# Sample attention of a hybrid decoder step: a batch's values move from behind the next batch's second quad of pages to behind its first, and ScalarE issues its pages one by one

## The chip, the cores and the metric

The kernel runs on one core of a Trainium2 chip. The metric is the device time of one execution in microseconds; the time before is the median of three runs.

## The reference, cut to what matters

The program is one inference step of a decoder layer (RWKV7 heads and MLA heads side by side, cross attention to a memory, a convolutional FFN) for a prompt of 1024 tokens and a sample group of 8 sequences with 4 new tokens each. The change concerns only the MLA attention of the sample group over its paged cache:

```python
lat_past = cache_mla_latent[l][page_table].reshape(Bs, past_len, KV_LORA)   # 8 x 2048 x 256
kr_past = cache_mla_krope[l][page_table].reshape(Bs, past_len, QK_ROPE)     # 8 x 2048 x 32
q_abs = jnp.einsum('bthd,chd->bthc', q_nope, w_uk)
sc_past = jnp.einsum('bthc,bsc->bhts', q_abs, lat_past) + jnp.einsum('bthr,bsr->bhts', q_rope, kr_past)
sc = jnp.concatenate([sc_past.astype(jnp.float32) * MLA_SCALE, sc_new], axis=-1)
pr = jax.nn.softmax(sc, axis=-1).astype(lat_new.dtype)
o_lat = (jnp.einsum('bhts,bsc->bthc', pr[..., :P], lat_past)
         + jnp.einsum('bhts,bsc->bthc', pr[..., P:], lat_new))
```

A sequence ("batch" in the code, 8 of them) has 16 pages of 128 positions. 8 heads times 4 tokens make 32 query rows.

## The kernel before

The kernel is a chain of stages, each a block in which every engine has a program of its own, written out by hand and tied to the others by semaphores; a stage begins when all engines have left the one before. The sample attention is `mla_sample_stage`. All is in float32.

Pages come by DMA into `keys` (latents) and `kr` (rotated keys), which hold two batches, `b % 2`. Three queues issue them, SyncE's, GpSimd's and ScalarE's; `LOADED` says which of the 16 pages each takes. Each page costs the issuing engine a load of the page's number from the table (`value_load`) and two issues, 16 KB of `kr` and 128 KB of `keys`. The pages of batch b+1 overwrite those of batch b-1, so all three wait for `o_made`, which TensorE counts up at the end of `outputs(b-1)`.

Four pages make a quad, four quads a batch. For quad n of batch b TensorE runs

- `transposes(b, n)`: eight 128x128 transposes of latents into two PSUM banks,
- `rope_keys(b, n)`: one transpose of the quad's rotated keys into slot n of the bank `xb`,
- `scores(b, n)`: the products with the queries, after ScalarE has copied the transposed quad out (`copy_keys`, two copies, and `copy_rope`, one).

When all four quads of batch b have scores, a chain follows that goes from engine to engine: VectorE takes the maximum (`maximum`, L1196 to L1200), TensorE spreads it over the partitions (`spread_maxima`, L1040 and L1041), VectorE reduces it (L1204), ScalarE takes the exponentials (`exponential`, L1136 and L1138), TensorE transposes them (`probabilities`, L1048 and L1050, into the same bank `xb`, all four slots), ScalarE copies them (`copy_probabilities`, L1143), and TensorE multiplies them with the pages (`outputs`, "the values", L1059 and L1061). VectorE copies the result (L1216), TensorE turns it (`turn_outputs`, L1066 and L1068), and VectorE scales it (L1218, L1221).

Each engine takes its instructions in the order of its program. Before the change TensorE's order for a batch b after the first is: quad 0 transposed; the last scores of b-1; quad 1 transposed; `spread_maxima(b-1)`; scores of quad 0; `probabilities(b-1)` and `outputs(b-1)`; quad 2 transposed; scores of quad 1; `turn_outputs(b-1)`; quad 3 transposed; scores of quad 2. ScalarE's order is: copies of quads 0 and 1; exponentials and copy of the probabilities of b-1; copies of quad 2; its three pages of batch b+1, all at once; copies of quad 3.

VectorE has other work in this stage. After the outputs of b-1 are scaled, it runs `shift` for two of the 14 tiles of RWKV's token shift (L1185 to L1191, two instructions over 1056 columns and two small ones each), and only then comes `maximum(b)`. There is no shift in the last batch.

Of the kernel before, what the change touches and what calls it, by code (L numbers as in the profile page):

```python
# [24 lines left out]
TP, NB, TSEQ = 1024, 8, 4  # L25
# [15 lines left out]
NPG = PAST // PAGE  # L41
# [850 lines left out]
def mla_sample_stage(k, free_y, free_cq, qabs, qrope):  # L892
# [7 lines left out]
    nc, io = k.nc, k.io  # L900
    R = NH * TSEQ
    GP, GC, NQ = 4, 4 * PAGE, NPG // 4
# [2 lines left out]
        "tr_made", "tr_taken", "t_made", "t_taken", "s_made", "gm", "rm", "dm", "b_made", "m_ready", "e_done", "l_sum", "l_diag",  # L905
        "pn_made", "pn_taken", "pt_made", "pt_taken", "o_made", "o_taken", "ot_made", "r_done", "ot_taken", "uv_made")}

    LOADED = (0, 2, 5, 8, 10, 13, 15), (1, 4, 6, 9, 12, 14), (3, 7, 11)
    k_in = [[[k.sem(f"ms_k{e}{j}{g}") for g in range(NQ)] for j in range(2)] for e in "spa"]
    loads = [[2 * sum(n in mine for n in range(GP * g, GP * (g + 1))) for g in range(NQ)] for mine in LOADED]  # L910
    B = k.bank
    lat = k.cqkv[:, QK:QK + KK, :]
# [7 lines left out]
    with ExitStack() as ctx:  # L920
# [3 lines left out]
        pages = k.sb(ctx, "ms_pages", [1, NB * NPG], I32)  # L924
# [21 lines left out]
        o_tr, l_ps = yb[:, 384:384 + KK * R], yb[:, 448:448 + R]  # L946
        query = lambda kk, b: qabs[:, kk, b, :, :].rearrange("p h t -> p (h t)")

        def load_batch(eng, e, b, j):
            for n in LOADED[e]:  # L950
                page = eng.value_load(pages[0:1, bass.ds(b * NPG + n, 1)], min_val=0, max_val=io["lat"].shape[0] - 1)
                eng.dma_start(kr[:, j, n, :], io["kr"][bass.ds(page, 1)].rearrange("a p c -> p (a c)"))\
                   .then_inc(k_in[e][j][n // GP], 16)
                eng.dma_start(keys[:, j, n, :], io["lat"][bass.ds(page, 1)].rearrange("a p c -> p (a c)"))\
                   .then_inc(k_in[e][j][n // GP], 16)

        def load_keys(eng, e):
            eng.wait_ge(S["pg"], 16)

            def load(b, j):  # L960
                load_batch(eng, e, b, j)
            load(0, 0)
            load(1, 1)
            with eng.Fori(1, NB // 2) as i:
                for j in range(2):

                    eng.wait_ge(S["o_made"], 2 * i + j - 1)
                    load(2 * i + j, j)
        with nc.Block() as block:
# [17 lines left out]
            def _(pe):  # L987
# [12 lines left out]
                def transposes(b, n):  # L1000
                    j, i = b % 2, NQ * b + n
                    for e in range(3):

                        pe.wait_ge(k_in[e][j][n], 16 * loads[e][n] * (b // 2 + 1))
                    if i >= 2:
                        pe.wait_ge(S["t_taken"], 2 * (i - 1))
                    for kk in range(KK):
                        for g in range(GP):
                            mm = pe.transpose(B[2 * (n % 2) + kk][:, g * PAGE:(g + 1) * PAGE],
                                              keys[:, j, GP * n + g, kk * P:(kk + 1) * P], ident)  # L1010
                        mm.then_inc(S["t_made"], 1)

                def rope_keys(b, n):
                    i = NQ * b + n
                    if i:
                        pe.wait_ge(S["tr_taken"], i)
                    if b and n == 2:
                        pe.wait_ge(S["pt_taken"], b)
                    pe.transpose(xb[:, n * P:(n + 1) * P],
                                 kr[:, b % 2, GP * n:GP * (n + 1), :].rearrange("p a c -> p (a c)"), ident).then_inc(S["tr_made"], 1)  # L1020

                def scores(b, n):
                    j, i, ps = b % 2, NQ * b + n, sbank[b % 2]
                    if n == 0 and b >= 2:
                        pe.wait_ge(S["e_done"], 2 * (b - 1))
                    pe.wait_ge(S["tr_taken"], i + 1)
                    pe.wait_ge(S["t_taken"], 2 * (i + 1))
                    c = slice(n * PAGE, (n + 1) * PAGE)
                    for kk in range(KK):
                        for g in range(GP):  # L1030
                            pe.matmul(ps[g * R:(g + 1) * R, c], query(kk, b), kT[:, n % 2, kk, g * PAGE:(g + 1) * PAGE],
                                      start=(kk == 0), stop=False, skip_group_check=True)
                    pe.matmul(ps[:, c], qd[:, b, :, :].rearrange("p g r -> p (g r)"), krT[:, j, c], start=False, stop=True,
                              skip_group_check=True).then_inc(S["s_made"], 1)
# [8 lines left out]

                def probabilities(b):
                    j = b % 2
                    pe.wait_ge(S["tr_taken"], NQ * b + 6 if b < NB - 1 else NQ * NB)
                    pe.wait_ge(S["e_done"], 2 * (b + 1))
                    pe.transpose(pn_ps, sc[:, j, GC:], ident).then_inc(S["pn_made"], 1)  # L1048
                    for n in range(NQ):
                        mm = pe.transpose(xb[:, n * P:(n + 1) * P], sc[:, j, n * PAGE:(n + 1) * PAGE], ident)  # L1050
                    mm.then_inc(S["pt_made"], 1)
# [20 lines left out]
                pe.wait_ge(S["nk"], 1)  # L1072
                pe.wait_ge(S["big"], 1)
                for b in range(NB):
                    transposes(b, 0)
                    rope_keys(b, 0)
                    if b:
                        scores(b - 1, NQ - 1)
                    transposes(b, 1)
                    rope_keys(b, 1)  # L1080
                    if b:
                        spread_maxima(b - 1)
                    else:
                        pe.wait_ge(S["qd"], GP)
                    scores(b, 0)
                    if b:
                        probabilities(b - 1)
                        outputs(b - 1)
                    transposes(b, 2)
                    rope_keys(b, 2)  # L1090
                    scores(b, 1)
                    if b:
                        turn_outputs(b - 1)
                    transposes(b, 3)
                    rope_keys(b, 3)
                    scores(b, 2)
                scores(NB - 1, NQ - 1)
                spread_maxima(NB - 1)
                probabilities(NB - 1)
# [11 lines left out]
            @block.scalar  # L1111
            def _(act):
                act.activation(kr0[:, :], k.krope[64:96, TP:T], ACT.Copy).then_inc(S["kr0"], 1)
                act.wait_ge(S["pg"], 16)
                load_batch(act, 2, 0, 0)
                act.wait_ge(S["qd_zero"], 1)
                for g in range(GP):
                    act.activation(qd[g * R:(g + 1) * R, :, g, :], qrope[:, :, :, :].rearrange("p b h t -> p b (h t)"), ACT.Copy)\
                       .then_inc(S["qd"], 1)

                def copy_keys(b, n):
                    i = NQ * b + n
                    for kk in range(KK):
                        act.wait_ge(S["t_made"], KK * i + kk + 1)
                        act.activation(kT[:, n % 2, kk, :], B[2 * (n % 2) + kk], ACT.Copy).then_inc(S["t_taken"], 1)

                def copy_rope(b, n):
                    act.wait_ge(S["tr_made"], NQ * b + n + 1)
                    act.activation(krT[:, b % 2, n * P:(n + 1) * P], xb[:, n * P:(n + 1) * P], ACT.Copy).then_inc(S["tr_taken"], 1)

                def exponential(b):
                    j = b % 2
                    act.wait_ge(S["m_ready"], b + 1)
                    if b:
                        act.wait_ge(S["l_sum"], b)
                    act.activation(sc[:, j, 0:GC], sbank[j], ACT.Exp, bias=stat[:, 2:3], scale=SCALE, accum_out=stat[:, 3:4])\  # L1136
                       .then_inc(S["e_done"], 1)
                    act.activation(sc[:, j, GC:], nsc[:, b * R:(b + 1) * R], ACT.Exp, bias=stat[:, 2:3], scale=SCALE,  # L1138
                                   accum_out=stat[:, 4:5]).then_inc(S["e_done"], 1)

                def copy_probabilities(b):
                    act.wait_ge(S["pt_made"], b + 1)
                    act.activation(pT[:, :], xb, ACT.Copy).then_inc(S["pt_taken"], 1)  # L1143
                load_batch(act, 2, 1, 1)
                act.wait_ge(S["nsc"], 1)
                for b in range(NB):
                    for n in range(NQ):
                        if b and n == 2:
                            exponential(b - 1)
                            copy_probabilities(b - 1)  # L1150
                        copy_keys(b, n)
                        copy_rope(b, n)
                        if n == 2 and 1 <= b < NB - 1:
                            act.wait_ge(S["o_made"], b)
                            load_batch(act, 2, b + 1, (b + 1) % 2)
                exponential(NB - 1)
                copy_probabilities(NB - 1)

# [1545 lines left out]
```

## Time and profile before

| | |
|---|---|
| time, median of 3 runs | 2604.76 us (2602.73 to 2605.34) |
| profiled execution, its own time | 2603.54 us |
| span of the profile | 2601.9 us |
| sample attention stage | about 605 to 757 us of the span |
| TensorE busy over the span | 2280.0 us (88%) |
| mean granted TensorE clock | 0.918 of full speed |

The profile gives times from the start of the span. Busy time of TensorE is its matrix products with modelled ends; "idle before" in a row is the time in which the engine did nothing before that instruction, with what ended it.

### The profile page before, as it was taken

What the parts mean: (1) busy time and instruction counts of PE and PEld (TensorE: products, weight loads), DVE (VectorE), ACT (ScalarE), POOL (GpSimd) and SP (SyncE); (2) the same over time, 40 slices, a digit from 0 to 9 for tenths busy, and PEclk for the clock granted to TensorE, in tenths of its full rate; (3) what the DMA queues carried; (4) which work ended last, traced back from release to release, by engine and by line L of the source; (5) the groups of instructions that cost most, each with busy time, mean ns of one, the idle gap of its engine ahead of it and who ended that gap; (6) DMA issues with size and microseconds to landing.
All of it is one profiled execution on the core that took longest, in us unless ns stands there. A gap on an engine that the chain in (4) does not pass through costs nothing. (4 is left out here: it accounts for less than half of the span.)

```text
span 2601.9 us, 51029 instructions
## 1 busy us (share of the span) xinstructions
PE 2280.0 (88%) x20442; PEld 2073.2 (80%) x20442; DVE 1317.5 (51%) x2428; ACT 649.8 (25%) x1340; POOL 285.6 (11%) x225
## 2 busy tenths in 40 slices
PE   5999589997763999977877899798999999999994
PEld 5999367776541899953776898798999999999994
DVE  5111644443547555535634224355666666666667
ACT  3000233443431444410223012112122222111212
POOL 2333000003313000000310310130000000000000
PEclk9999799998985999975898898899999999999997
DMA  3110100004520000010314124201111111111112
GB/s 131 49 45 27 37 11 11 11 1 112 145 60 0 8 4 4 4 40 0 123 41 131 71 73 148 79 33 55 49 48 43 49 50 49 50 41 50 33 33 73
DMA packets 79018, 131.55 MB, mean 51 GB/s; under 512 B 26705, under 2 KB 56274, under 8 KB 78706
## 3 DMA queue, kind: packets, MB, share of 16 engines
q1 hardware_dynamic: 67698, 117.12, 13.6%
q0 software_dynamic: 4224, 8.13, 1.2%
q10 hardware_dynamic: 6912, 3.54, 0.5%
q8 instruction: 153, 2.51, 0.4%
q14 instruction: 31, 0.25, 0.0%
HBM read 119.48 MB, written 9.29 MB: 49 GB/s over the span
## 5 line engine op out<-in xcount | busy, mean ns | idle before, releaser
L345 PE MATMUL psum<-high,ff_up 128*128 128x352 f32 x2112 | 517.5, 326 | 4.9 <-DVE ff_u L2439 3.1
L345 PEld LDWEIGHTS psum<-high,ff_up 128*128 128x128 f32 x2112 | 370.6, 189 | 7.1 <-DVE ff_u L2439 4.3
L345 PE MATMUL psum<-low,ff_up 128*128 128x352 f32 x1056 | 341.1, 323 | 0.0
L345 PE MATMUL psum<-hid,ff_down 128*128 128x352 f32 x1584 | 259.6, 325 | 12.1 <-issue 12.1
L345 PEld LDWEIGHTS psum<-hid,ff_down 128*128 128x128 f32 x1584 | 258.0, 189 | 12.4 <-issue 12.4
L345 PE MATMUL psum<-h_high,pj_part 128*128 128x352 f32 x960 | 236.0, 327 | 30.4 <-POOL pj_part L396 24.7
L345 PEld LDWEIGHTS psum<-low,ff_up 128*128 128x128 f32 x1056 | 199.5, 189 | 0.0
L345 PEld LDWEIGHTS psum<-h_high,pj_part 128*128 128x128 f32 x960 | 172.1, 192 | 31.1 <-POOL pj_part L396 24.7
L2484 DVE TENSOR_TENSOR x<-x,psum 128x352 f32<-128x352 f32 x264 | 137.2, 521 | 114.8 <-PE psum L345 114.8
L345 PE MATMUL psum<-h_low,pj_part 128*128 128x352 f32 x480 | 157.7, 328 | 0.0
L2334 ACT ACTIVATE ff_up<-ff_slot 128x1024 fp32r<-128x1024 f32 x44 | 46.2, 1051 | 390.9 <-PE psum L345 384.7
L345 PE MATMUL psum<-high,wo_part 128*128 128x352 f32 x384 | 95.7, 331 | 12.1 <-POOL wo_part L396 11.1
L345 PE MATMUL psum<-m_high,mo_part 128*128 128x352 f32 x384 | 94.9, 329 | 9.5 <-POOL mo_part L396 9.5
L2365 ACT ACTIVATE ff_c<-ff_u,vecs 128x1072 f32<-128x1072 f32 x44 | 56.5, 1285 | 185.8 <-DVE ff_u L2439 146.9
L345 PE MATMUL psum<-m_high,mq_part 128*128 128x352 f32 x384 | 95.2, 330 | 3.9 <-POOL mq_part L396 3.9
L1484 PE MATMUL psum<-rc_W 64*64 64x64 f32 x1296 | 90.5, 222 | 3.5 <-DVE rc_W L1592 2.6
L486 DVE TENSOR_TENSOR rw<-psum,acc 128x352 f32 x42 | 22.1, 526 | 140.4 <-PE psum L345 140.4
L345 PEld LDWEIGHTS psum<-h_low,pj_part 128*128 128x128 f32 x480 | 91.9, 191 | 0.1
L716 PEld LDWEIGHTS psum<-mp_v,mp_pT 128*128 128x128 f32 x576 | 71.8, 195 | 21.3 <-issue 11.4
L716 PE MATMUL psum<-mp_v,mp_pT 128*128 128x64 f32 x576 | 76.2, 279 | 7.0 <-ACT mp_pT L787 7.0
L345 PEld LDWEIGHTS psum<-high,wo_part 128*128 128x128 f32 x384 | 68.9, 193 | 13.5 <-POOL wo_part L396 12.2
L834 DVE TENSOR_REDUCE mp_stat<-psum 128x1 f32<-128x128 f32 (+3 forms) x64 | 48.4, 756 | 58.0 <-PE psum L696 57.9
(395 smaller groups left out, 4605.2 us busy)
## 6 DMA issues: line engine op xcount, KB each, us to landing
ff_slot<-in_w_up SPq DMA_DIRECT2D x44, 512.0 KB, 3.3
ff_slot<-in_w_down SPq DMA_DIRECT2D x22, 512.0 KB, 3.2
pj_slot<-in_w_in SPq DMA_DIRECT2D x20, 512.0 KB, 3.2
mk_slot<-in_w_mkv SPq DMA_DIRECT2D x16, 512.0 KB, 3.3
mz_k<-in_memk SPq DMA_DIRECT2D x8, 1024.0 KB, 5.5
mz_v<-in_memv SPq DMA_DIRECT2D x8, 1024.0 KB, 7.5
ms_keys<-in_lat SPq DMA_DIRECT2D x56, 128.0 KB, 2.7
ms_keys<-in_lat POOLq DMA_DIRECT2D x48, 128.0 KB, 3.0
```

What stands on the lines that cost most here:

```text
L345: mm = pe.matmul(ps, w(a, kk), rhs(b, kk), start=(kk == 0 and n == 0), stop=(kk == nk - 1 and n == 2))
L486: return eng.tensor_tensor(dst[:, bass.ds(m, 1), n * C3:(n + 1) * C3], ps.unsqueeze(1), third(k.acc, n).unsqueeze(1), ALU.mult)
L716: mm = pe.matmul(B[6][:, 0:HD], pT[:, i % 2, t * P:(t + 1) * P], v[:, t, h * HD:(h + 1) * HD], start=(t == 0), stop=(t == i))
L834: dve.reduce_max(mx[:, i:i + 1], ps, AX).then_inc(S["maxed"], 1)
L1484: mm = pe.matmul(PV[hf][h, at(64 * q)], W[h, p, N_, :], W[h, p, TT_, :], start=True, stop=True)
L2334: act.activation(dst[:, 0], slot[:, j], ACT.Copy).then_inc(S["w_high"], 1)
L2365: act.activation(cv[:, j, :], u[:, j, 2:U], ACT.Identity, bias=k.vecs[:, bass.ds(b0, 1)], scale=k.vecs[:, bass.ds(w2, 1)]).then_inc(S["c_f ...
L2484: dve.tensor_tensor(xs, xs, B[4 + g % 4][:, 0:C3], ALU.add).then_inc(S["down_taken"], 1)
```

## The change

On TensorE the last scores of batch b-1 and `spread_maxima(b-1)` come first, ahead of quad 0 of batch b. Then quad 0 is transposed, and `probabilities(b-1)` and `outputs(b-1)` follow at once. Quad 1 is transposed after them, then come the scores of quad 0 and `turn_outputs(b-1)`, and quads 2 and 3 in the plain order. On ScalarE the exponentials of b-1 come ahead of the copies of quad 0, and the copy of the probabilities behind them. Its three pages of b+1 are issued one each behind the copies of quads 1, 2 and 3. Pages are dealt to the queues anew: ScalarE's are 7, 11 and 15 (3, 7 and 11 before), SyncE and GpSimd share the others. The semaphore values follow the new order: `probabilities(b)` waits for the rope copy of quad 0 of b+1 (quad 1 before).

```diff
-    LOADED = (0, 2, 5, 8, 10, 13, 15), (1, 4, 6, 9, 12, 14), (3, 7, 11)
+    LOADED = (0, 2, 4, 6, 9, 12, 14), (1, 3, 5, 8, 10, 13), (7, 11, 15)
...
-                    if b and n == 2:
+                    if b and n == 1:
                         pe.wait_ge(S["pt_taken"], b)
...
-                    pe.wait_ge(S["tr_taken"], NQ * b + 6 if b < NB - 1 else NQ * NB)
+                    pe.wait_ge(S["tr_taken"], NQ * b + 5 if b < NB - 1 else NQ * NB)
...
                 for b in range(NB):
+                    if b:
+                        scores(b - 1, NQ - 1)
+                        spread_maxima(b - 1)
                     transposes(b, 0)
                     rope_keys(b, 0)
                     if b:
-                        scores(b - 1, NQ - 1)
+                        probabilities(b - 1)
+                        outputs(b - 1)
+                    else:
+                        pe.wait_ge(S["qd"], GP)
                     transposes(b, 1)
                     rope_keys(b, 1)
-                    if b:
-                        spread_maxima(b - 1)
-                    else:
-                        pe.wait_ge(S["qd"], GP)
                     scores(b, 0)
                     if b:
-                        probabilities(b - 1)
-                        outputs(b - 1)
-                    transposes(b, 2)
-                    rope_keys(b, 2)
-                    scores(b, 1)
-                    if b:
                         turn_outputs(b - 1)
-                    transposes(b, 3)
-                    rope_keys(b, 3)
-                    scores(b, 2)
+                    for n in range(2, NQ):
+                        transposes(b, n)
+                        rope_keys(b, n)
+                        scores(b, n - 1)
...
                 for b in range(NB):
-                    for n in range(NQ):
-                        if b and n == 2:
-                            exponential(b - 1)
-                            copy_probabilities(b - 1)
+                    if b:
+                        exponential(b - 1)
+                    copy_keys(b, 0)
+                    copy_rope(b, 0)
+                    if b:
+                        copy_probabilities(b - 1)
+                    for n in range(1, NQ):
                         copy_keys(b, n)
                         copy_rope(b, n)
-                        if n == 2 and 1 <= b < NB - 1:
-                            act.wait_ge(S["o_made"], b)
-                            load_batch(act, 2, b + 1, (b + 1) % 2)
+                        if 1 <= b < NB - 1:
+                            if n == 1:
+                                act.wait_ge(S["o_made"], b)
+                            load_page(act, 2, b + 1, (b + 1) % 2, LOADED[2][n - 1])
```

`load_page` is the body of the old `load_batch` for one page.

## Rows read from the trace of the kernel before

**Rows 1.** The page of the profile, its first line.

```profile
span 2601.9 us, 51029 instructions
```

**Rows 2.** Busy time of each engine, six batches' period and the stage's end.

```profile
core 0: us, PE busy (x) PEld busy (x) DVE busy (x) ACT busy (x) POOL busy (x), PEclk, DMA share, GB/s
...
632.30:735.20 102.90, 80.34 (x944) 59.52 (x943) 51.04 (x114) 40.09 (x102) 38.70 (x72) 0.97 0.53 141
735.20:756.50 21.30, 15.55 (x160) 10.84 (x159) 4.82 (x17) 4.19 (x11) 0.00 (x0) 0.73 0.09 21
```

**Rows 3.** Waits of TensorE, 632.3 to 735.2: us, times, longest.

```profile
PE psum L1009 <- DMA ms_keys<-in_lat: 8.4, 6, 2.5
...
PE psum L1009 <- ACT ms_kT L1125: 2.1, 1, 2.1
```

**Rows 4.** Timeline of one undisturbed period: start, us, engine line op, idle before.

```profile
667.20 1.09 PE L1009 MATMUL psum<-masks,ms_keys 128*128 128x128 f32 x8
667.31 0.43 DVE L1216 COPY ms_ol<-psum 128x256 f32<-128x256 f32 x1 [3.50 <-PE psum L1061]
667.89 1.08 ACT L1125 ACTIVATE ms_kT<-psum 128x512 f32<-128x512 f32 x2 [3.33 <-PE psum L1009]
...
668.86 0.28 ACT L1129 ACTIVATE ms_krT<-psum 128x128 f32<-128x128 f32 x1
...
669.23 0.31 PE L1066 MATMUL psum<-ms_ld,masks 128*128 128x32 f32 x2
...
670.62 1.25 DVE L1185 TENSOR_TENSOR sh_tmp<-rw 128x1055 f32<-128x1055 f32 x1
...
676.08 0.68 DVE L1196 TENSOR_REDUCE ms_stat<-psum 128x1 f32<-128x512 f32 x1
...
678.43 0.69 ACT L1136 ACTIVATE ms_sc<-psum,ms_stat 128x512 f32<-128x512 f32 x1
...
679.65 0.27 PE L1048 MATMUL psum<-masks,ms_sc 128*32 128x128 f32 x1 [0.59 <-ACT ms_sc L1138]
...
681.14 1.93 PE L1059 MATMUL psum<-ms_keys,ms_pT 128*32 128x256 f32 x32 [0.78 <-ACT ms_pT L1143]
...
683.73 0.42 DVE L1216 COPY ms_ol<-psum 128x256 f32<-128x256 f32 x1 [3.50 <-PE psum L1061]
```

**Rows 5.** Timeline of a period that waited for pages.

```profile
639.31 1.97 PE L1009 MATMUL psum<-masks,ms_keys 128*128 128x128 f32 x8 [2.27 <-DMA ms_keys<-in_lat]
...
643.00 0.69 DVE L1196 TENSOR_REDUCE ms_stat<-psum 128x1 f32<-128x512 f32 x1 [1.79 <-PE psum L1033]
```

**Rows 6.** ScalarE's page issues in the timeline.

```profile
669.11 0.34 ACTq L952 DMA_DIRECT2D ms_kr<-in_kr  x1
...
670.67 0.34 ACTq L952 DMA_DIRECT2D ms_kr<-in_kr  x1
```

**Rows 7.** GpSimd's second page in the timeline, and landing time of latent pages.

```profile
671.01 0.54 POOL L954 DMA_DIRECT2D ms_keys<-in_lat  x1
```

```profile
DMA to landing us min/median/max: 2.0/3.0/4.3
```

**Rows 8.** Timeline of the last batch's chain.

```profile
741.00 0.69 DVE L1196 TENSOR_REDUCE ms_stat<-psum 128x1 f32<-128x512 f32 x1 [2.32 <-PE psum L1033]
...
742.26 0.49 PE L1040 MATMUL psum<-ms_dm,masks 128*128 128x128 f32 x2 [1.30 <-DVE ms_dm L1200]
...
744.56 0.27 PE L1048 MATMUL psum<-masks,ms_sc 128*32 128x128 f32 x1 [1.59 <-ACT ms_sc L1138]
...
746.23 3.64 PE L1059 MATMUL psum<-ms_keys,ms_pT 128*32 128x256 f32 x32 [0.78 <-ACT ms_pT L1143]
...
751.06 0.42 DVE L1216 COPY ms_ol<-psum 128x256 f32<-128x256 f32 x1 [5.91 <-PE psum L1061]
```

**Rows 9.** Stretches of 1 us; the columns are those of rows 2.

```profile
639.00:640.00 1.00, 0.69 (x3) 0.69 (x4) 0.96 (x4) 0.72 (x3) 0.54 (x2) 0.57 0.59 136
...
708.00:709.00 1.00, 0.18 (x2) 0.19 (x3) 1.00 (x2) 0.82 (x2) 0.20 (x2) 1.00 0.68 191
```

More of the change, by code:

```diff
@@ L947, in mla_sample_stage, with load_page @@
         query = lambda kk, b: qabs[:, kk, b, :, :].rearrange("p h t -> p (h t)")
[L949 to L955, printed above, removed]
+        def load_page(eng, e, b, j, n):
+            page = eng.value_load(pages[0:1, bass.ds(b * NPG + n, 1)], min_val=0, max_val=io["lat"].shape[0] - 1)
+            eng.dma_start(kr[:, j, n, :], io["kr"][bass.ds(page, 1)].rearrange("a p c -> p (a c)"))\
+               .then_inc(k_in[e][j][n // GP], 16)
+            eng.dma_start(keys[:, j, n, :], io["lat"][bass.ds(page, 1)].rearrange("a p c -> p (a c)"))\
+               .then_inc(k_in[e][j][n // GP], 16)
         def load_keys(eng, e):
@@ L960, in load @@
             def load(b, j):
-                load_batch(eng, e, b, j)
+                for n in LOADED[e]:
+                    load_page(eng, e, b, j, n)
             load(0, 0)
@@ L1114, in _ @@
                 act.wait_ge(S["pg"], 16)
-                load_batch(act, 2, 0, 0)
+                for n in LOADED[2]:
+                    load_page(act, 2, 0, 0, n)
                 act.wait_ge(S["qd_zero"], 1)
@@ L1143, in copy_probabilities @@
                     act.activation(pT[:, :], xb, ACT.Copy).then_inc(S["pt_taken"], 1)
-                load_batch(act, 2, 1, 1)
+                for n in LOADED[2]:
+                    load_page(act, 2, 1, 1, n)
                 act.wait_ge(S["nsc"], 1)
                 for b in range(NB):
-                    for n in range(NQ):
-                        if b and n == 2:
-                            exponential(b - 1)
-                            copy_probabilities(b - 1)
+                    if b:
[5 more added lines that the diff above has]
+                    for n in range(1, NQ):
                         copy_keys(b, n)
                         copy_rope(b, n)
-                        if n == 2 and 1 <= b < NB - 1:
-                            act.wait_ge(S["o_made"], b)
-                            load_batch(act, 2, b + 1, (b + 1) % 2)
+                        if 1 <= b < NB - 1:
+                            if n == 1:
+                                act.wait_ge(S["o_made"], b)
+                            load_page(act, 2, b + 1, (b + 1) % 2, LOADED[2][n - 1])
                 exponential(NB - 1)
```

## Prediction

> **What bounds the kernel now.** I read the first line of the page for the span to which all is added [rows 1], then cut the stage into stretches with the view of busy time, listed TensorE's waits in the middle stretch, and followed one period instruction by instruction in the timeline. Nothing outside the stage is touched, and the next stage starts when this one ends, so what the stage gains or loses the program gains or loses.
>
> The stretch from 632.3 to 735.2 us runs from the copy of batch 0's outputs to that of batch 6: six periods in 102.9 us, a mean of 17.15 us, of which TensorE is busy 13.4 us [rows 2]. So TensorE stands still for 3.8 us a period. Of those 22.6 us in all, 8.4 us are waits for pages and 2.1 us one wait for ScalarE's copies, which its page issues held up [rows 3]. The rest is the chain: each period it waits 0.59 us for the exponentials and 0.78 us for the copied probabilities [rows 4].
>
> The reader should see two halves in a period. I count from the copy of the outputs (v, 667.31 us), which is when pages may be loaded. The first half ends at VectorE's maximum at 676.08 us, 8.77 us later. That row has no idle before it: VectorE comes straight from the two shifts that began at 670.62 us, so in an undisturbed period VectorE's shifts, not the pages, say when the maximum starts. The second half is the chain from the maximum to the next copy of outputs at 683.73 us, 7.65 us. Together 16.42 us [rows 4]. In a period disturbed by pages the maximum came at 643.00 us, 10.7 us after v at 632.3, and did wait for TensorE [rows 2, 5]. Two periods are of this kind; four of nearly 16.5 us and two of 18.4 us make the 102.9.
>
> **What the change takes away.** Pages of b+1 are still issued from v on, but the values are now ahead of quad 1, so at v three quads of b are left instead of two, before b+1 is touched. The fourth page of a batch is now GpSimd's second; that issue came 3.7 us after v, and with the longest landing time of 4.3 us it is there at v + 8.5 [rows 4, 7]. TensorE asks for it only behind the maximum's spreading, at about v + 10.6 (below). The page waits go, 8.4 us. What they were worth is less: it is the excess of the two disturbed periods, 2 x 1.9 = 3.8 us, since in the others VectorE would not have started earlier anyway.
>
> **ScalarE's pages.** Issues of consecutive pages are 1.56 us apart [rows 6]. One page between two quads' copies therefore makes ScalarE's quad about 2.1 us (0.5 us until the second copy is under way and its sequencer is free, and 1.6), against TensorE's quad of 2.03 us (667.20 to 669.23) [rows 4]. It holds the last scores up by 0.1 us or so, at most by one issue, 1.6 us, if an issue is slow. The last scores end near v + 7.7 and VectorE is free at v + 8.77, so 1.0 us of it is covered by the shifts. I take nothing.
>
> **What the change puts on the path.** VectorE's order is unchanged. `turn_outputs` still comes one quad behind the values, hence the shifts still begin 3.3 us after v and the maximum still starts at v + 8.77. The shifts that were half hidden by page waits are now the bound of every first half.
>
> The second half gets longer. `probabilities` overwrites the bank `xb`, in whose slot 0 the rope keys of b+1's first quad stand, and so waits for their copy. ScalarE now makes the three copies of that quad behind the exponentials. In the period shown, exponentials start at 678.43 and `probabilities` at 679.65. Between the two there will now stand one set of copies, from 667.89 to 668.86 + 0.28 = 1.25 us [rows 4]. A copy of this quad cannot be earlier: ScalarE's program has it behind `exponential`. The lower bound is 1.2 us and the upper, if TensorE's transposes of the quad are late too, 1.9. I take 1.22, at the lower end: the quad is transposed 1.8 us after the spreading begins, and the exponentials end only 2.2 us after it. The second half is then 7.65 + 1.22 = 8.87 us, and the period 8.77 + 8.87 = 17.64 us.
>
> Six periods: 6 x 17.64 = 105.8 against 102.9: +2.9 us. The last batch has no shift, but at v one more quad is left than before: +2.03 us [rows 4]. In batch 0 the last scores now come ahead of a quad, which starts the chain some 1.0 us sooner, and the 1.2 us of copies follow: +0.2 us. The end of the stage, from the last maximum at 741.00 us on, is as it was. Sum at an unchanged clock: +5.1 us.
>
> **The clock.** TensorE now stands still while the chain runs. Before, quads lay in the gaps; now, from the end of the last scores (v + 7.6) it waits 2.4 us for the maximum (v + 8.77, and 1.26 us more to the spreading, as 741.00 to 742.26 shows [rows 8]), works 1.8 us on the spreading and quad 0, waits some 1.7 us for the copies, works 0.7 us and waits 0.8 us. About 4.9 us of 7.5 are idle, every batch.
>
> The trace shows what such stretches do. Before the disturbed period TensorE was idle for 2.27 us; the granted clock sank from 1.00 within that microsecond (mean 0.57), and the eight transposes took 1.97 us instead of 1.09 [rows 5, 9]. In the last batch it waited 1.30 us and 1.59 us with the spreading between; the products of the values then ran at 1.2 GHz, 3.64 us instead of 1.93, and from their start to the copy of the outputs went 4.83 us instead of 2.59 [rows 4, 8]. Against that stands the wait of 2.1 us, after which the clock was still 1.00 [rows 3, 9]; but quads ran on both sides of it. The new period has a longer gap than any of these and a second one 1.8 us of work later. So I expect the clock to fall in nearly every batch.
>
> What a fall costs depends on what it covers. If only the spreading and quad 0: the transposes take 0.9 us more, part of it behind the exponentials, so about 0.6 us. If the values: 4.83 - 2.59 = 2.2 us. If both and the quad after: 2.2 + 0.6 with some 0.5 for the first transposes, about 3. Seven batches have this chain with a quad in it (0 to 6). Both kinds should occur; in the middle between 0.6 and 2.2, 1.5 us each, so 7 x 1.5 = +10.5 us (bounds +4 and +21).
>
> The Trainium skill, "TensorE: Matmul & The Clock Gate", speaks to this in two places. Its section "HAM oscillation" ties a fall to a single long wait of TensorE, longer than any gap worked out above; by it there would be none here and +5.1 us would stay. The trace speaks against it: the clock fell behind a wait of 2.27 us. Its section "A second HAM failure mode: psum-queue depth-cycling" says that frequent short idling between groups of matmuls is enough to make the clock swing; the falling clock in the last batch agrees.
>
> **The sum.** Against the profiled execution: its span is 2601.9 us and its time 2603.54, the median is 1.2 us more than that time. +5.1 and +10.5 make +15.6 us: 2619.1 for the profiled execution, 2620.4 against the median of 2604.76. Slower by 0.6%.
>
> **The rivals.**
> (a) The clock holds: 2609.9 us, just inside 0.2%. For it: the wait of 2.1 us that it survived. Against it: both falls above, and two gaps in each period. Chance 0.15.
> (b) The shifts do not hold the maximum up. Then the first half is about 7.7 us, the period 16.6, six periods 99.5: 3.4 us won, 2.2 lost at both ends, 2603.6 at an unchanged clock. Against it: no idle before the maximum's row in the undisturbed period, and VectorE's order is untouched. Chance 0.05.
> (c) Faster: the copies of quad 0 stay off the path between exponentials and probabilities, because TensorE and ScalarE pass it while VectorE is still at work. This is worth 6 x 1.22 = 7.3 us, and the period would be 16.42; with 2.0 us lost at the end 6 x 16.42 = 98.5 gives -4.4 + 2.0 = -2.4 us, and with (b) as well -8.6 us, 2596.2. It turns faster by 0.2% only from 0.5 us less per period than 16.42. The program order on ScalarE and the wait for `xb` stand against it. Chance 0.03.
> (d) The change does not do what it says: page waits remain, since pages came up to 2.5 us late before [rows 3]. They would have to exceed the 2 us of reserve for quad 0 and add to the forecast: 2625 us. Within the forecast's range.
>
> **Chances and range.** Forecast 0.77 (with (d)), its own range 2611 to 2628. Below 2608 lie (b) and (c), above 2629 falls that cover the values and more in every batch: together under 0.2. Range 2608 to 2629. A measurement of this kernel can tell about 0.2%, 5.2 us, from no change. Faster: (c), 0.03. Same: (b) and a little over half of (a), 0.14. Slower: 0.83.
>
> **What would show it.** In the new profile: waits of TensorE for pages near zero between batch 0's and batch 6's outputs; a period of 17.6 us plus what the clock costs, so that the stretch of six becomes 112 to 120 us; VectorE's maximum again 8.8 us after the copy of outputs, with no idle before it; ScalarE's copies of quad 0 straight behind the exponentials, and TensorE waiting for the rope copy ahead of `probabilities`, some 1.7 us; `spread_maxima` behind a wait of 2.4 us for VectorE; and a granted clock under 1.00 in the chain of most batches, with values taking up to 3.64 us. The prediction is wrong if the clock stays at 1.00 in the stretch, or if the maximum starts well before v + 8.77.

## The result, and the profile after

The changed kernel takes 2611.85 us (median of 20 runs, 2603.87 to 2621.09) against 2600.39 us for the kernel before (20 runs on the same chips, 2592.19 to 2608.41): 11.5 us more, ratio 1.0045 with a 95% interval of 1.0035 to 1.0054. It is slower, as forecast, and inside the range. The forecast difference was 15.6 us. The absolute time forecast, 2620.4 us, also stood on the first three runs of before, whose median is 4.4 us over that of all 20.

```profile
span 2606.6 us, 51030 instructions
```

The profiled execution is 4.7 us longer than that of before [rows 1], which hides more than it shows. From VectorE's first use of the new tokens' scores to its last copy of the stage went 147.8 us before (608.04 to 755.85) and 157.4 us now (604.17 to 761.53), 9.6 us more. The stage began 3.9 us earlier, by an earlier stage that the change doesn't touch, and what follows the stage took 1.0 us less. So I read the stage, and take the whole from the medians.

The view of busy time, from the copy of batch 0's outputs to that of batch 6; columns as in [rows 2]:

```profile
630.07:739.22 109.15, 82.27 (x943) 60.91 (x944) 50.91 (x115) 39.49 (x102) 38.55 (x72) 0.94 0.52 137
```

Six periods take 109.15 us instead of 102.9, and the granted clock is 0.94 instead of 0.97. The waits of TensorE from 623 to 740 us:

```profile
PE psum L1040 <- DVE ms_dm L1203: 15.5, 7, 2.4
PE psum L1048 <- ACT ms_krT L1127: 9.7, 7, 1.7
PE psum L1059 <- ACT ms_pT L1141: 5.4, 7, 0.8
```

This list answers to [rows 3]. All waits for pages are gone, 8.4 us of them. In their place stand 15.5 us for VectorE's maximum ahead of the spreading and 9.7 us for the rope copy ahead of `probabilities`. These count seven chains; in the six periods of [rows 3] alone the two are 14.2 and 8.0 us. A period in which the clock held, in the timeline (compare [rows 4]; VectorE's and ScalarE's line numbers have moved by a few):

```profile
648.10 0.42 DVE L1219 COPY ms_ol<-psum 128x256 f32<-128x256 f32 x1 [3.50 <-PE psum L1061]
...
656.87 0.68 DVE L1199 TENSOR_REDUCE ms_stat<-psum 128x1 f32<-128x512 f32 x1
...
658.12 0.49 PE L1040 MATMUL psum<-ms_dm,masks 128*128 128x128 f32 x2 [2.36 <-DVE ms_dm L1203]
...
659.20 0.69 ACT L1134 ACTIVATE ms_sc<-psum,ms_stat 128x512 f32<-128x512 f32 x1 [4.55 <-DVE ms_stat L1207]
...
660.18 1.07 ACT L1123 ACTIVATE ms_kT<-psum 128x512 f32<-128x512 f32 x2
...
661.13 0.28 ACT L1127 ACTIVATE ms_krT<-psum 128x128 f32<-128x128 f32 x1
...
661.47 0.28 PE L1048 MATMUL psum<-masks,ms_sc 128*32 128x128 f32 x1 [1.65 <-ACT ms_krT L1127]
...
665.57 0.42 DVE L1219 COPY ms_ol<-psum 128x256 f32<-128x256 f32 x1 [3.50 <-PE psum L1061]
```

The maximum starts 8.77 us after the copy of outputs, to the hundredth what it was, and again without idle time before it. From there to the next copy of outputs go 8.70 us, 1.05 us more than in [rows 4], and the copies of quad 0 (660.18 to 661.41) stand in that stretch. The period is 17.47 us.

The other periods were 18.03, 19.11, 17.98 and 19.09 us. What they have more, 4.3 us in all, is falls of the granted clock from 2.4 to 1.2 GHz. Two of them in the timeline; the answers in before are the fall in [rows 8] and the slow transposes in [rows 5]:

```profile
640.15 0.79 PE L1040 MATMUL psum<-ms_dm,masks 128*128 128x128 f32 x2 [2.40 <-DVE ms_dm L1203]
...
641.16 1.91 PE L1009 MATMUL psum<-masks,ms_keys 128*128 128x128 f32 x8
...
735.00 3.03 PE L1059 MATMUL psum<-ms_keys,ms_pT 128*32 128x256 f32 x32 [0.78 <-ACT ms_pT L1141]
...
739.22 0.42 DVE L1219 COPY ms_ol<-psum 128x256 f32<-128x256 f32 x1 [5.11 <-PE psum L1061]
```

Behind a gap of 2.40 us the spreading took 0.79 us instead of 0.49 and quad 0 took 1.91 us; such a period is 0.5 us longer. Where the fall came later, the values took 3.03 us instead of 1.93, and the period is 1.6 us longer. The granted clock in one microsecond of those values is 0.50 (columns as in [rows 2]):

```profile
737.00:738.00 1.00, 1.00 (x13) 0.19 (x5) 0.00 (x0) 0.00 (x0) 0.00 (x0) 0.50 0.68 150
```

### The profile page after: what moved, and what is told of

The parts are those of the page before. It is cut to its first block and busy times, and to the rows that moved or that the text cites. A ratio compares the mean times of both kernels' runs of the same rounds, so it can differ in the third digit from the quotient of the medians.

```text
span 2606.6 us, 51030 instructions
## 1 busy us (share of the span) xinstructions
PE 2277.4 (87%) x20442; PEld 2070.9 (79%) x20442; DVE 1317.4 (51%) x2428; ACT 648.6 (25%) x1340; POOL 285.5 (11%) x225
## 3 DMA queue, kind: packets, MB, share of 16 engines
q1 hardware_dynamic: 67698, 117.12, 13.5%
## 5 line engine op out<-in xcount | busy, mean ns | idle before, releaser
L345 PEld LDWEIGHTS psum<-hid,ff_down 128*128 128x128 f32 x1584 | 257.8, 189 | 12.4 <-issue 12.4
```

The lines of the kernel that those rows point to most:

```text
L345: mm = pe.matmul(ps, w(a, kk), rhs(b, kk), start=(kk == 0 and n == 0), stop=(kk == nk - 1 and n == 2))
```

## The experiments

Theory: VectorE's shifts fix the first half of a period, the copies of quad 0 lengthen the second, and with no quads left inside the chain TensorE's clock falls in it. Rivals: pages or ScalarE's issues still hold the kernel; the loss is all waits and the clock costs nothing; what matters is how ScalarE issues. Every kernel was measured beside the kernel before on its chip. The ratios are to that, and "before us" is its median there.

| run | median us | before us | ratio (95%) | copies of outputs of batches 0 to 6, us |
|---|---|---|---|---|
| the change | 2611.85 | 2600.39 | 1.0045 (1.0035 to 1.0054) | 109.15 |
| e1, after, no reload | 2607.96 | 2598.51 | 1.0048 (1.0029 to 1.0068) | 109.44 |
| e2, before, no reload | 2609.40 | 2598.51 | 1.0042 (1.0028 to 1.0056) | 114.46 |
| e3, after, narrow filler | 2616.12 | 2598.51 | 1.0058 (1.0039 to 1.0077) | 111.74 |
| e4, after, quad 0 first | 2616.16 | 2598.51 | 1.0065 (1.0049 to 1.0080) | 118.15 |
| e5, after, shift moved | 2604.51 | 2600.49 | 1.0017 (0.9999 to 1.0035) | 106.56 |
| e6, before, shift moved | 2600.42 | 2600.49 | 0.9994 (0.9983 to 1.0005) | 105.42 |
| e7, after, issue in one | 2624.09 | 2600.49 | 1.0080 (1.0058 to 1.0102) | 128.32 |
| e8, before, issue one by one | 2604.71 | 2600.49 | 1.0007 (0.9995 to 1.0020) | 108.01 |
| e9, after, transposes in the gaps | 2599.68 | 2600.01 | 0.9996 (0.9982 to 1.0009) | 104.91 |
| e10, quad 0 first and shift moved | 2599.12 | 2600.01 | 0.9992 (0.9978 to 1.0005) | 103.18 |
| e11, e10 with transposes | 2586.54 | 2600.01 | 0.9945 (0.9926 to 0.9964) | 92.58 |
| e12, before, transposes | 2601.14 | 2601.06 | 0.9994 (0.9978 to 1.0009) | 103.99 |

**e1: are pages still on the path?**

```diff
-            with eng.Fori(1, NB // 2) as i:
-                for j in range(2):
-                    eng.wait_ge(S["o_made"], 2 * i + j - 1)
-                    load(2 * i + j, j)
...
-                        pe.wait_ge(k_in[e][j][n], 16 * loads[e][n] * (b // 2 + 1))
+                        pe.wait_ge(k_in[e][j][n], 16 * loads[e][n])
...
-                        if 1 <= b < NB - 1:
-                            if n == 1:
-                                act.wait_ge(S["o_made"], b)
-                            load_page(act, 2, b + 1, (b + 1) % 2, LOADED[2][n - 1])
```

> The changed kernel without the loads of pages for batches 2 to 7 on all three queues (and without their waits): it computes with the pages of batches 0 and 1 again. Theory (shifts on VectorE and the chain set the period, pages hidden): the time of the changed kernel, 11.5 us over before, within 2 us; periods of 17.5 us plus falls of the clock. Rival (pages or ScalarE's page issues still hold the changed kernel): 5 us or more faster than the changed kernel.

No. Without the reloads the ratio is the changed kernel's, and the six periods too. The maximum still starts at v + 8.77 us in each. Pages and ScalarE's issues are hidden in the changed kernel. (e1 and e2 compute with stale pages, so only their times mean anything.)

**e2: what were the page waits worth before?** The same edit on the kernel before.

> The kernel before, without the loads of pages for batches 2 to 7 (and without their waits): it computes with the pages of batches 0 and 1 again. Theory (waits for pages were worth only the excess of the late periods over the shifts on VectorE): periods of 16.4 us, 3.8 to 4.5 us faster than before. Rival (each wait of TensorE for pages was on the path): 10.5 us faster than before.

Both were wrong: taking the waits away cost 10.9 us. In the view of busy time the granted clock fell to 0.81 over the six periods:

```profile
622.52:736.98 114.46, 93.73 (x943) 66.82 (x944) 50.82 (x115) 40.40 (x102) 0.00 (x0) 0.81 0.02 5
```

and the timeline of one period says why:

```profile
672.89 0.49 PE L1035 MATMUL psum<-ms_dm,masks 128*128 128x128 f32 x2 [2.38 <-DVE ms_dm L1192]
...
677.19 3.64 PE L1054 MATMUL psum<-ms_keys,ms_pT 128*32 128x256 f32 x32 [0.78 <-ACT ms_pT L1138]
```

With pages at hand TensorE transposes quads 0 and 1 early and then waits 2.38 us for VectorE, which in four of the six periods still starts its maximum at v + 8.77 us (in the other two, behind a slow chain, at v + 10.3 and 10.6). Before, the idle time lay in waits ahead of quads, six for pages of 8.4 us in all [rows 3], and quad 1 stood between the maximum and the spreading. The idle time has moved into the chain, as in the changed kernel, and in four of the six periods the values ran at 1.2 GHz: 3.64 us. TensorE's waits in the six periods sum to 20.8 us against 22.6 us before, so here it counted more where the waiting lay than how much of it there was.

**e3: TensorE kept busy with narrow products.**

```diff
+                def fill(count):
+                    for _ in range(count):
+                        pe.matmul(B[3][:, 0:32], ident, ident[:, 0:32], start=True, stop=True, skip_group_check=True)
...
                         scores(b - 1, NQ - 1)
+                        fill(14)
                         spread_maxima(b - 1)
...
                     rope_keys(b, 0)
                     if b:
+                        fill(9)
                         probabilities(b - 1)
```

> The changed kernel with 14 products of 128x32 that nobody reads ahead of the spreading and 9 ahead of the probabilities, in a free bank, so that TensorE is busy in its two long gaps. Theory (falls of the clock make up what the median of the changed kernel has over the sum of its waits, 4 to 8 us): the clock stays at 1.00 in the six periods, each 17.5 us, and the time is 4 to 8 us under the changed kernel's, so 4 to 8 us over before. Rival (the whole loss is the chain and the shifts; the clock costs nothing): the time of the changed kernel, 11.5 us over before.

It did not do what it was made for. The filler overran the first gap, so that an undisturbed period was 18.1 us, and two falls remained in the six periods:

```profile
665.91 3.21 PE L1038 MATMUL psum<-masks 128*128 128x32 f32 x28
...
673.88 3.55 PE L1063 MATMUL psum<-ms_keys,ms_pT 128*32 128x256 f32 x32 [0.78 <-ACT ms_pT L1147]
```

The microseconds around the start of the values, columns as in [rows 2]:

```profile
673.00:674.00 1.00, 0.22 (x5) 0.15 (x8) 0.00 (x0) 0.60 (x1) 0.00 (x0) 1.00 0.00 0
674.00:675.00 1.00, 1.00 (x13) 0.58 (x12) 0.00 (x0) 0.00 (x0) 0.00 (x0) 0.52 0.00 0
```

TensorE has no gap in these rows but the last, 0.78 us ahead of the values, which the filler left open; the clock was still 1.00 while that gap lasted and fell to 1.2 GHz right behind it, in both falls. Whether the narrow products or the open gap let it fall can't be told from this run. By itself it left the clock's share open too; e9 goes further.

**e4: quad 0 into the gap ahead of the spreading.**

```diff
-                        spread_maxima(b - 1)
                     transposes(b, 0)
                     rope_keys(b, 0)
                     if b:
+                        spread_maxima(b - 1)
                         probabilities(b - 1)
...
-                    if b:
-                        exponential(b - 1)
                     copy_keys(b, 0)
                     copy_rope(b, 0)
                     if b:
+                        exponential(b - 1)
                         copy_probabilities(b - 1)
```

> The changed kernel with quad 0 of the next batch transposed ahead of the spreading of the maxima, and its copies on ScalarE ahead of the exponentials. Theory (copies of quad 0 between exponentials and probabilities cost 1.2 us a batch, and the gap of 2.4 us ahead of the spreading lets the clock fall): the second half of a period is 7.65 us instead of 8.7, the period 16.4 us, the time 2 us under before (14 us under the changed kernel). Rival 1 (pages of quad 0 are now asked for 7.7 us after the copy of outputs and are late): waits for pages of up to 1 us a batch come back, and where VectorE's shifts do not cover them the time is 2 to 4 us over before. Rival 2 (the copies cost nothing): the time of the changed kernel less the clock's share.

The copies left the path, yet the time is 17.65 us over before's. The six periods took 118.15 us at a mean clock of 0.80:

```profile
630.54:748.69 118.15, 95.64 (x943) 66.14 (x944) 50.87 (x114) 40.50 (x102) 38.55 (x72) 0.80 0.47 126
```

One chain:

```profile
682.15 0.49 PE L1040 MATMUL psum<-ms_dm,masks 128*128 128x128 f32 x2 [1.37 <-DVE ms_dm L1202]
...
684.45 0.37 PE L1048 MATMUL psum<-masks,ms_sc 128*32 128x128 f32 x1 [1.58 <-ACT ms_sc L1136]
...
686.45 3.64 PE L1059 MATMUL psum<-ms_keys,ms_pT 128*32 128x256 f32 x32 [0.78 <-ACT ms_pT L1141]
```

No wait is longer than 1.6 us, and no page is late. But between 1.37, 1.58 and 0.78 us of waiting there is only the spreading and five transposes, and the values took 3.64 us in five of the six periods and 3.39 in the other. In three periods the next quad ran at 1.2 GHz too, the last scores came late, and the maximum with them (v + 10.3 to 10.8 instead of 8.8). My expectation had the waits right and left out the clock.

**e5 and e6: VectorE's shifts.**

```diff
                         total(b - 1)
+                        if b < NB - 1:
+                            shift(2 * b, 0)
                         take_outputs(b - 1)
+                    else:
+                        shift(2 * b, 0)
                     if b < NB - 1:
-                        shift(2 * b, 0)
                         shift(2 * b + 1, 1)
```

> The changed kernel with the first of a batch's two shifts on VectorE ahead of the copy of outputs, in the time in which VectorE waits for the values; the second stays behind the scaled outputs. Theory (the two shifts set the start of the maximum 8.8 us after the copy of outputs, TensorE would be ready at 7.7): the maximum starts at 7.7 us, a period is 1.0 us shorter, six of them 6 us; the gap ahead of the spreading shrinks from 2.4 to 1.3 us, so falls of the clock become fewer; 6 to 9 us under the changed kernel, 2.5 to 5.5 over before. Rival (the shifts only fill a wait): the time of the changed kernel, 11.5 us over before.

> The kernel before with the same move of one shift. Theory: in its undisturbed periods TensorE ends the last scores only 0.3 us before the maximum starts, held by pages and copies, so it gains 0.3 us in each of four or five periods, 1 to 2 us under before. Rival (the shifts hold before by as much as the changed kernel): 6 us under before.

On the changed kernel the maximum now waits for TensorE, 7.7 us after the copy of outputs (664.32):

```profile
672.04 0.69 DVE L1199 TENSOR_REDUCE ms_stat<-psum 128x1 f32<-128x512 f32 x1 [1.60 <-PE psum L1033]
```

Its shortest period is 16.41 us, 1.06 less than 17.47, and the time is 7.3 us under the changed kernel's. Falls are left (the other periods are 16.9 to 19.4 us). On the kernel before, three maxima start 0.3 us sooner (v + 8.46 to 8.48), as the theory said, but the time does not show it: the ratio's interval runs from 4.4 us under to 1.3 us over before. The rival's 6 us is excluded, the theory's 1 to 2 us can't be told from none. So the shifts do set the first half in the new order, and in the old one pages and copies stand close behind them.

**e7 and e8: how ScalarE issues.** e7 puts the old split and the block of three issues back into the changed kernel:

```diff
-                        if 1 <= b < NB - 1:
-                            if n == 1:
-                                act.wait_ge(S["o_made"], b)
-                            load_page(act, 2, b + 1, (b + 1) % 2, LOADED[2][n - 1])
+                        if n == 1 and 1 <= b < NB - 1:
+                            act.wait_ge(S["o_made"], b)
+                            for m in LOADED[2]:
+                                load_page(act, 2, b + 1, (b + 1) % 2, m)
```

> The changed kernel with the old split of the pages over the queues and ScalarE's three pages issued at once behind the copies of quad 1. Only TensorE's order and ScalarE's order of copies are then changed. Theory (ScalarE's issues matter by the slack of 1.0 us of the shifts): the block of three issues takes 4.0 us, the copies of quad 2 start 1.5 us late, those of quad 3 follow at once and the last scores end at most 0.5 us later than in the changed kernel, all under the shifts; the time of the changed kernel within 2 us. Rival (issuing one by one is a gain of its own in this order): 1 us a batch, 6 us over the changed kernel.

> The kernel before with the new split of the pages and ScalarE's pages issued one each behind the copies of quads 2 and 3 and of the next batch's quad 0; TensorE's order as before. Theory: the copies of quad 3 are no longer 2.3 us late, but the pages of the next quad 0 (GpSimd's second now) land no earlier and TensorE asks for them as early as before, so at most the 2.1 us wait for copies goes; 0 to 3 us under before. Rival (ScalarE's block of issues was what held the old order): 6 us or more under before.

e7 was the largest miss: 12 us over the changed kernel, where I had expected nothing. The timeline:

```profile
652.76 1.78 ACTq L953 DMA_DIRECT2D ms_keys<-in_lat  x1
...
656.13 1.09 ACT L1123 ACTIVATE ms_kT<-psum 128x512 f32<-128x512 f32 x2 [5.54 <-PE psum L1009]
...
657.45 0.33 PE L1019 MATMUL psum<-masks,ms_kr 128*128 128x128 f32 x1 [1.99 <-ACT ms_krT L1127]
```

The view of busy time and TensorE's largest wait, both from the copy of batch 0's outputs to that of batch 6:

```profile
626.18:754.50 128.32, 99.94 (x943) 70.47 (x944) 51.40 (x115) 39.28 (x102) 38.70 (x72) 0.77 0.43 116
```

```profile
PE psum L1019 <- ACT ms_krT L1127: 8.8, 6, 2.0
```

In every one of the six periods TensorE stood in front of a quad until ScalarE had done with its three issues and copied, 0.92 to 1.99 us, where the changed kernel does not wait at all. The row above is the longest of them, with one issue of 1.78 us instead of 0.34; it is ScalarE's only issue over 0.6 us in these periods, so it is the block as such that holds the copies up, and the slow issue adds to it once. The maximum started 9.7 to 12.4 us after the copy of outputs, not at 8.77. The shortest period, 18.37 us, is 0.9 us over the changed kernel's 17.47, which makes 5.4 of the 19.2 us that the six periods are longer; the others are 20.8 to 24.4 us, and the mean clock is 0.77, so much of the loss came by the clock once more. How much was not separated.

So the one-by-one issue is a part of the change that pays, by 9 us going by the ratios (1.0080 and 1.0045) and 12 by the medians, but only in this order: on the kernel before it brings nothing that can be measured (e8: the interval runs from 1.3 us under to 5.2 over before). The wait for the copies is gone there, as the theory said, but TensorE's waits for pages grew from 8.4 to 14.6 us. e7 differs in the split of the pages too. That was not tried by itself, but TensorE has no wait for a page in the six periods of e7, so the split didn't hold it there.

**e9: TensorE kept busy with full transposes.** As e3, with

```diff
+                        pe.transpose(B[3][:, 0:P], ident, ident)
```

for the product, 17 times ahead of the spreading, 12 ahead of the probabilities, 5 ahead of the values. Nobody reads the bank's content.

```profile
634.05:738.96 104.91, 98.47 (x1147) 79.06 (x1148) 50.92 (x114) 39.59 (x102) 38.70 (x72) 1.00 0.53 141
```

The granted clock is 1.00 over the whole stretch and the periods are 17.47 to 17.53 us, each. The kernel does more work than the changed one, waits for the same things, and is 12 us faster (ratios 0.9996 and 1.0045). With the falls gone, all that the change had lost is won back.

That doesn't make the longer waits free. The kernel before has falls of its own, e9 has hardly any, and the comparison sets the one against the other. The mean granted clock over the whole program shows it: 0.9205 for before (mean of the 81 runs recorded beside the experiments), 0.9184 for the change, 0.9228 for e9. Among the runs of before, 0.001 less of it goes with 1.6 us more time. By that, as an estimate, e9 would be about 4 us over before at before's own clock, close to the +5.1 us that the prediction gave the waits. A single profiled pair can't show this: those of the change and of e9 took 2608.24 and 2606.59 us, 3.6 under and 6.9 over their medians.

**e10 and e11: a kernel that is faster than both.** e10 is e4 and e5 together, with pages 2 and 3 exchanged between ScalarE and SyncE. e11 adds 12 and 5 transposes ahead of probabilities and values.

```diff
-    LOADED = (0, 2, 4, 6, 9, 12, 14), (1, 3, 5, 8, 10, 13), (7, 11, 15)
+    LOADED = (0, 3, 5, 8, 10, 13, 15), (1, 4, 6, 9, 12, 14), (2, 7, 11)
...
                         spread_maxima(b - 1)
+                        fill(12)
                         probabilities(b - 1)
+                        fill(5)
```

> The changed kernel with both: quad 0 transposed ahead of the spreading with its copies ahead of the exponentials, and one shift moved ahead of the copy of outputs; page 2 goes to ScalarE and page 3 to SyncE, so that quad 0's pages are issued sooner. By the waits alone a period is 7.7 + 7.6 = 15.3 us, 13 us less for six than the changed kernel's 17.5. Theory (the chain now holds hardly any matrix work, and the clock falls in each batch for longer, as with quad 0 alone, where periods were 18 to 21 us): periods of 17 to 19 us, time 4 to 12 us over before. Rival (with the shift out of the way the gaps are short enough): periods of 15.3 to 16 us, time 6 to 10 us under before.

> The kernel of e10_quad0_and_shift with 12 unread transposes ahead of the probabilities and 5 ahead of the values. Theory (only the clock keeps that order from its 15.3 us): the clock stays at 1.00 in the six periods, 15.3 to 15.8 us each, so 92 to 95 us for six against 103 before; 6 to 10 us under before. Rival (pages of quad 0, asked for 7.6 us after the copy of outputs, are late): waits for pages in TensorE's rows of 0.5 to 2 us a batch, periods of 16 to 17.5 us, time from 6 us under before to 2 over.

The view of busy time over the six periods, e10 and then e11:

```profile
628.52:731.70 103.18, 86.81 (x943) 61.10 (x944) 48.59 (x110) 40.29 (x102) 38.57 (x72) 0.88 0.54 142
```

```profile
629.83:722.41 92.58, 87.26 (x1045) 68.02 (x1046) 48.61 (x111) 40.19 (x102) 38.57 (x72) 1.00 0.58 156
```

e10 has periods of 16.9 to 17.2 us at a clock of 0.88 (the first 18.2), the low end of the theory's, and ends level with before, not 4 us or more over it. e11 differs from it by the transposes alone and has 15.34 to 15.38 us after the first, 15.77, at a clock of 1.00: 13.5 us under before, more than the 6 to 10 expected. One of its chains:

```profile
668.67 0.69 DVE L1204 TENSOR_REDUCE ms_stat<-psum 128x1 f32<-128x512 f32 x1 [1.60 <-PE psum L1033]
...
672.24 0.27 PE L1052 MATMUL psum<-masks,ms_sc 128*32 128x128 f32 x1 [0.28 <-ACT ms_sc L1142]
...
673.72 1.93 PE L1063 MATMUL psum<-ms_keys,ms_pT 128*32 128x256 f32 x32 [0.23 <-ACT ms_pT L1147]
```

The sum by waits, 15.3 us, comes out to within 0.1 us once the clock is held, and pages are not late.

**e12: do such transposes help any order?** The kernel before with 4 and 5 of them in its two short gaps, in bank `B[1]`, which is free there.

> The kernel before with unread transposes in the two short gaps of its chain: 4 ahead of the probabilities and 5 ahead of the values, in a bank that is free there. Theory (before has quads between its gaps, its clock falls only behind late pages, where these transposes do not stand): falls as before, 0 to 2 us under before. Rival (unread transposes help any order by as much, 12 us as in the changed kernel): 6 us or more under before.

No: 0.9994, with an interval from 5.7 us under to 2.3 us over before; the theory's 0 to 2 us can't be told from none. The old order has quads in its chain, and its two longest periods, 18.3 and 19.0 us, are again those in which the maximum waited for a late TensorE, ahead of which these transposes do not stand.

## Why the prediction was right, point by point

- **VectorE's shifts bound the first half.** Right. v + 8.77 us in all six periods of the changed kernel and in e1; moving one shift takes 1.06 us off (e5).
- **Page waits go, and were worth 3.8 us only.** The waits went. Their worth, 3.8 us, is not shown: e2 can't tell it, because without them the clock fell more often. That the step could have no price apart from the clock was not seen.
- **ScalarE's single issues cost nothing.** Right for the change as made (e1). The sentence did not go on to say what the block of issues would have cost; e7 shows 9 to 12 us, falls of the clock included.
- **The copies of quad 0 on the path.** Forecast 1.22 us and a period of 17.64; measured 1.05 and 17.47. From the exponentials' start to `probabilities` go 2.27 us instead of 1.22: ScalarE is on to the copies after 0.98 us, so the hand-over to TensorE within the 1.22 is paid once, not twice.
- **The unchanged-clock sum, +5.1 us.** Its size fits, its parts don't. In the profiled stages e9, the changed kernel at full clock up to the last batch's chain, took 152.7 us (607.00 to 759.74) against 147.8: +4.9 us. Of these, 2.0 lie in the six periods (2.9 forecast), 2.7 ahead of the copy of batch 0's outputs (0.2 forecast) and 0.2 behind that of batch 6 (2.0 forecast: the quad that is left did bring the last maximum 1.97 us later, but the chain behind it was 1.1 us shorter than before's, and the rest of the stage 0.6 us). That they add up to the forecast is luck, and each rests on one profiled execution. By e9's ratio the new order is 4.7 us under to 2.3 us over before, since before pays for falls of its own; at equal clock the estimate above gives 4 us.
- **The clock, +10.5 us.** That the clock costs this much is shown by e9: 12 to 13 us, by medians and ratios. The profiled executions show less. The falls of the six periods cost 4.3 us, and the stages of the change and of e9 are 4.6 us apart: four falls at 0.5 or 1.6 us each, the two kinds that were forecast, in four of six periods instead of all. The price of one was right for the first kind (0.6) and 0.6 us too high for the second (2.2), since such a fall covered only a part of the values. What the falls were in the executions that make the medians can't be seen.
- **Rival (a), the clock holds.** Refuted. The Trainium skill, "TensorE: Matmul & The Clock Gate", section "HAM oscillation", ties falls to one long wait; here no wait of the six periods was over 2.40 us and the clock of e4 fell with none over 1.6 us. The section "A second HAM failure mode: psum-queue depth-cycling" of the same page of the Trainium skill, which names frequent short idling between groups of matmuls, agrees with both.
- **Rivals (b), (c), (d).** (b) and (c) did not occur, but both are reachable: e10 removes the shifts and the copies from the path, and e11 shows that 15.3 us is what is then left. (d) did not occur: TensorE has no wait for a page left.

By medians and ratios the first term came out some 6 us lower than forecast (-4.7 to +2.3 us, as before has falls too) and the clock's some 2 us higher. That the sum, 15.6 against 11.5, came close is owed in part to these two errors going opposite ways. The mechanism is borne out by the rows.

## What to carry to other kernels

When a chain that goes from engine to engine is pulled together so that TensorE only waits and does small products in it, price the clock as well as the waits: here holding it gave back the whole measured loss. Before changing an order to take away a wait, ask where the idle time will go; several waits of 0.5 to 2.5 us between quads were cheaper than one of 2.4 us ahead of a chain, even with less work to do (e2). If the better order needs the gaps, unread 128x128 transposes in a free bank can hold the clock, as in e9 and e11; count them so that they end before the wait does. Where the falls lie behind late pages they bring nothing (e12).

## What the runs showed of the hardware

- With products of 128x32 in the first two gaps of the chain the clock still fell in two of six periods (e3); with transposes of 128x128 in all three it stayed at 1.00 (e9). The fillers differ in size and in the third gap, and which of the two counts is not shown.
- A fall that goes on into the next quad costs more: with values and that quad at 1.2 GHz e4's periods were 20.6 to 21.0 us, against 17.9 and 18.9 where the quad ran at full clock again.
- The issue of one 128 KB page from ScalarE takes 0.34 us nearly always, but single ones took 1.78 us (e7), 1.44 (e9) and 1.25 (e8), also where pages were issued one by one. In e7 an issue of SyncE that had begun 0.15 us earlier took 1.93 us. What makes them slow was not tried. The one of 1.44 us in e9 cost nothing: its period is 17.48 us like the others.
